# The low parts of three weight blocks move from GpSimd into VectorE's triangular inverse

## What is computed

```python
h = rms_norm(x, norm_g) * (1.0 + scale) + shift
proj = h @ w_in
pool_u, pool_g, q, k, v, ret_g, rw, rw_g, gate_logits = jnp.split(proj, points, axis=-1)
o_pool = causal_pool_mixer(pool_u, pool_w, pool_scale) * jax.nn.silu(pool_g)
o_ret = retention(q, k, v, positions, ret_norm_g) * jax.nn.silu(ret_g)
o_rwkv = rwkv7_time_mix(rw, ...) * jax.nn.silu(rw_g)
...
return x + gate * (merged @ w_out)
```

## Time and profile before

| | |
|---|---|
| three runs | 1833.15, 1835.55, 1838.32 us, median 1835.55 |
| the profiled execution | 1840.28 us, its span 1838.2 us |
| TensorE matmuls busy | 1718.2 us, 93% of the span |
| VectorE busy | 1036.0 us, 56% |
| ScalarE busy | 800.7 us, 44% |
| GpSimd busy | 632.0 us, 34% |
| granted TensorE clock, mean | 0.968 |

### The profile page before, as it was taken

How to read it: one execution, slowest core, us unless ns; L and a number is a source line. 1 busy time by engine, 2 the same in 40 slices (tenths; PEclk the granted TensorE clock), 3 DMA queues, 4 the chain that set the end, 5 groups by cost and what they waited for, 6 DMA issues and landing times. The chain is left out here.

```text
span 1838.2 us, 26011 instructions
## 1 busy us (share of the span) xinstructions
PE 1718.2 (93%) x10688; PEld 1373.8 (75%) x10688; DVE 1036.0 (56%) x1367; ACT 800.7 (44%) x1200; POOL 632.0 (34%) x344
## 2 busy tenths in 40 slices
PE   8999989999999899899999999989999999987783
PEld 6877778888888787688888888868888986544441
DVE  4346744666665325584556766443116627866675
ACT  2455522333223335542333222344337736866673
POOL 1336612424444434751243444433421021322210
PEclk7999989999999899998999999989999999999997
DMA  8223321215444323322122544333420067999994
GB/s 344 81 92 106 90 77 36 92 58 192 171 166 171 126 92 96 96 85 77 54 85 66 209 175 169 138 126 126 149 92 1 1 240 265 382 388 395 389 392 178
DMA packets 82605, 287.97 MB, mean 157 GB/s; under 512 B 30473, under 2 KB 30601, under 8 KB 65332
## 3 DMA queue, kind: packets, MB, share of 16 engines
q1 hardware_dynamic: 76708, 275.87, 41.6%
q0 software_dynamic: 5040, 8.25, 1.4%
q10 hardware_dynamic: 736, 2.14, 0.3%
HBM read 274.50 MB, written 22.61 MB: 162 GB/s over the span
## 5 line engine op out<-in xcount | busy, mean ns | idle before, releaser
L1525 POOL TENSOR_TENSOR wmem_r<-wmem,wmem_r 128x1024 fp32r<-128x1024 f32 x170 | 420.2, 2473 | 696.4 <-ACT wmem_r L1041 685.5
L721 PE MATMUL banks<-h_hi_r,wmem_r 128*128 128x512 f32 x1632 | 511.2, 392 | 6.9 <-POOL wmem_r L1525 6.9
L721 PEld LDWEIGHTS banks<-h_hi_r,wmem_r 128*128 128x128 f32 x1632 | 307.9, 189 | 77.0 <-POOL wmem_r L1525 9.4
L1041 ACT ACTIVATE wmem_r<-wmem 128x1024 fp32r<-128x1024 f32 x170 | 180.2, 1060 | 405.2 <-DMA wmem<-wstream 402.2
L721 PE MATMUL banks<-hT_r,wmem_r 128*128 128x512 f32 x816 | 319.0, 391 | 0.0
L721 PEld LDWEIGHTS banks<-hT_r,wmem_r 128*128 128x128 f32 x816 | 154.0, 189 | 31.3
L2725 DVE TENSOR_TENSOR slots_r<-slots,wmem_r 128x1024 fp32r<-128x1024 f32 x102 | 121.9, 1217 | 57.7 <-ACT wmem_r L2418 52.1
L2806 POOL TENSOR_TENSOR wmem_r<-wmem,wmem_r 128x1024 fp32r<-128x1024 f32 x30 | 74.8, 2493 | 202.3 <-ACT wmem_r L2276 202.3
L992 PE MATMUL banks<-slots_r,wmem_r 128*128 128x512 f32 x512 | 127.7, 389 | 0.0
L1465 DVE SCALAR_TENSOR_TENSOR ztp<-xT,c_act,ztp 128x256 f32<-128x256 f32 x168 | 122.8, 731 | 6.0
L741 PE MATMUL banks<-wmem_r,h_hi_r 128*128 128x512 f32 x384 | 118.9, 391 | 0.0
(11 more groups left out here) (450 smaller groups left out, 3043.1 us busy)
## 6 DMA issues: line engine op xcount, KB each, us to landing
wmem<-wstream SPq DMA_DIRECT2D x206, 512.0 KB, 3.3
slots<-experts SPq DMA_DIRECT2D x80, 1024.0 KB, 24.5
xT<-ada SPq DMA_DIRECT2D x24, 1024.0 KB, 5.8
xT<-experts SPq DMA_DIRECT2D x16, 1024.0 KB, 25.0
slots<-ada SPq DMA_DIRECT2D x8, 1024.0 KB, 18.0
x_keep<-xT SPq DMA_DIRECT2D x2, 2048.0 KB, 17.4
xT<-x_keep SPq DMA_DIRECT2D x2, 2048.0 KB, 8.1
dil_rows<-dil_once SPq DMA_DIRECT2D x1, 2560.0 KB
```

The costliest lines, as they stand in the source:

```text
L721: mm = nc.tensor.matmul(o, r(lhs[:, k, :]), r(rhs[:, k, :]), start=(k == 0 and i == 0), stop=(k == KD - 1 and i == 2))
L1041: inc(nc.scalar.activation(r(chunk(b)[0]), w, ACT.Copy), "w_high")
L1525: inc(g.tensor_tensor(r(lo), lo, r(hi), ALU.subtract), "w_split")
```

## The change

Three of the blocks, rg3 (25), tg0 (26) and tg1 (27), get their low part from VectorE: ahead of the turns i = 13, 20 and 27 of the inverse's loop. GpSimd leaves them out, and a new semaphore `v_split` counts them, for which TensorE waits in place of `w_split`. GpSimd still makes the low parts of rg0, rg1, rg2, tg2 and tg3.

```diff
+LOW_AT = {13: FIRST["rg"] + 3, 20: FIRST["tg"], 27: FIRST["tg"] + 1}
+BY_VECTOR = sorted(LOW_AT.values())
...
-        split_count = lambda b: b + 1 - sum(w <= b for w in WHOLE)
+        high_count = lambda b: b + 1 - sum(w <= b for w in WHOLE)
+        split_count = lambda b: high_count(b) - sum(w <= b for w in BY_VECTOR)
+        split_of = lambda b: ("v_split", BY_VECTOR.index(b) + 1) if b in BY_VECTOR else ("w_split", split_count(b))
...
-                after("w_split", split_count(b))
+                after(*split_of(b))
...
             for i in range(SUB - 1):
+                if i in LOW_AT:
+                    hi, lo = chunk(LOW_AT[i])
+                    after("w_high", high_count(LOW_AT[i]))
+                    inc(v.tensor_tensor(r(lo), lo, r(hi), ALU.subtract), "v_split")
...
-                    if b not in WHOLE:
-                        after("w_high", split_count(b))
+                    if b not in WHOLE and b not in BY_VECTOR:
+                        after("w_high", high_count(b))
```

More of the change, by code:

```diff
@@ L451, in program @@
                           ("o_sqrt", 1), ("ret_done", 4), ("gate_sig", 24), ("merged", 40),
-                          ("w_high", LAYER_B - len(WHOLE)), ("w_split", LAYER_B - len(WHOLE)), ("quarter_used", 9), ("h_high", 8),
+                          ("w_high", LAYER_B - len(WHOLE)), ("w_split", LAYER_B - len(WHOLE) - len(BY_VECTOR)), ("v_split", len(BY_VECTOR)), ("quarter_used", 9), ("h_high", 8),
                           ("br_high", 3), ("br_split", 3), ("m_high", 8), ("m_split", 8)):
@@ L733, in project_tok @@
                     at = FIRST[prefix] + b
-                    after("w_split", split_count(at))
+                    after(*split_of(at))
                     w = [part.rearrange("p (k n) -> p k n", k=2) for part in chunk(at)]
```

## The result

| kernel | median | range, runs | ratio to the kernel before, 95% interval |
|---|---|---|---|
| before | 1837.09 us | 1832.79 to 1839.87, 8 | |
| changed | 1845.47 us | 1840.99 to 1850.59, 8 | 1.0054 [1.0041, 1.0067] |
| changed, a second time | 1846.89 us | 1839.13 to 1849.53, 6 | 1.0061 [1.0042, 1.0080] |

The change makes the kernel slower: by 8.4 us, 0.46%, between the two medians, and by 0.54% in the ratio of the table. The forecast was 4.5 us, and 1840 us. The profiled execution of the changed kernel took 1844.64 us (span 1842.7 us), the one of before 1840.28 us.

A forecast was written before the change was run, and what follows sets the result against it. TensorE's matmuls, busy 93% of the span, were taken as the bound. Net lateness 9.5, plus 1.7 for a clock fall, minus 6.5 of clock returned gave +4.7 us: 1840 us from a median of 1835.55, range 1833 to 1847.

The forecast's parts named there:

- The low parts late: TensorE waits for VectorE's low parts at rg3, tg0 and tg1: 1.55, 2.14 and 3.3 us later, 7.0 us a layer.
- the rival price: By the shared read port rule, each low part on VectorE costs 2.1 us instead of 1.22; no chance given.
- One fall of the clock among dense matmuls: New idle times among the blocks lower TensorE's clock once in the two layers: 1.7 us lost, ends 0 and 3.4.
- What it gives back: Around `zp`: the waits ahead of it go, 2.63 and 1.87 us, and a higher clock returns 6.5 us.
- The covered wait: TensorE's wait ahead of `zp` for the inverse's spread disappears: 2.63 us in the first layer, 1.87 in the second.
- The clock: Without the wait the clock may stay up from `zp` on: 6.5 us back over both layers, ends 0 and 10.
- case 2: Clock falls during small tiles in `zp` and `zc`, wait or no wait: +9.5 to +13 us, 1845 to 1848.5; chance 0.22.
- I carry the difference over unchanged: The +4.7 us on the profiled execution (1840.3 to 1845.0) is applied to the median, 1835.55, giving 1840 us.
- Case 4: Low parts are in time, VectorE's loop running ahead of TensorE: 11 us faster, about 1824.5 us; chance 0.08.

The follow-up runs named there:

- changed, a second time: The changed kernel run again with nothing edited: 1846.89 us, ratio 1.0061 to the kernel before.
- The kernel with other turns: Changed kernel with the three low parts ahead of turns 8, 13 and 18 instead of 13, 20 and 27: 1836.27 us, 0.9997 of before.
- the held pair: Changed kernel and its variant with turns 8, 13 and 18, both with SyncE's three weight loads held until `zc`'s last product: 1844.44 and 1828.27 us.
- A: Not a run: the stretch in TensorE's timeline from rg2's first matmul to `py`, added over both layers; 65.55 us before, 80.89 us changed.
- With the loads held: Changed kernel with SyncE's three weight loads behind the inverse's spread held until `zc`'s last product: 1844.44 us, 1.0045 of before.
- B: Not a run: the stretch from `py` to step 0's first state-update product, added over both layers; 43.90 us before, 34.48 us changed.
- before, second: Second trace of the kernel before, nothing edited: 1835.53 us, ratio 0.9998.
- With them held in both kernels: SyncE's three weight loads held until `zc`'s last product, in the kernel before (1832.90 us) and with turns 8, 13 and 18 (1828.27 us).
- earlier turns for two of three: Changed kernel with rg3's and tg0's low parts at turns 8 and 13, tg1's still at 27: 1852.02 us, 1.0098 of before.
- extra matmuls: Kernel before with eight overwritten 128 x 512 matmuls filling TensorE's wait ahead of `zp`: 1837.75 us; with the three weight loads also held, 1830.83 us.

## Why the prediction fell short

**The low parts late: right.** The waits were said to be about 1.3, 1.9 and 3.1 us, with VectorE as the releaser; they are 1.17, 1.76 and 3.00. The subtraction takes 1.23 us (1.22 said, and 2.1 by the rival price). Late by 7.0 us a layer: from rg2 to `py` the first layer has 39.63 - 32.77 = 6.9 us more. The kernel with other turns shows that it is the place and not the work, and the held pair prices it in the whole kernel's time.

**One fall of the clock among dense matmuls: right,** in either trace, in one layer of the two; A shows it at 1.5 to 1.6 us. With the loads held there were two, so that it was one is partly luck.

**What it gives back: mis-sized,** and this is the step that failed. The forecast took the full wait ahead of `zp`, 2.63 + 1.87 = 4.5 us, and 6.5 us of clock, 11.0 in sum. By two traces of each kernel B falls from (43.90 + 42.63) / 2 = 43.27 to (34.48 + 38.21) / 2 = 36.35 us, that is 6.9 us. With A's 15.34 this makes +8.4 us, the difference first measured (the second was 11.7). The start of `zp` in the timelines cuts B in two. All columns are us, summed over both layers:

| trace | `py` to `zp` | `zp` to the update | full clock lost | idle, issue named |
|---|---|---|---|---|
| before | 17.25 | 26.65 | 13.6 | 1.35 |
| before, second | 14.78 | 27.85 | 6.8 | 5.84 |
| changed | 12.61 | 21.87 | 3.4 | 2.06 |
| changed, second | 12.60 | 25.61 | 8.5 | 3.09 |

- The covered wait, the first column: 3.4 us on average where 4.5 were taken. One execution of before showed waits of 4.5 us, another 2.0, and `zp` starts 6.3 us behind `py` in all four layers of the changed kernel.
- The clock, the second column, which has the late instructions in it too: 3.5 us where 6.5 were taken. The forecast read 13.6 us of lost clock from one execution, and another of the same kernel has half of it. It also let the clock stay up once the wait was gone. No layer of the changed kernel has a wait ahead of `zp`, and the clock falls in `zc` in three of four. What lowers it there is open: it did so with stalls and, with the loads held, without.
- The late instructions, for which there was no term: 1.35 and 5.84 us of such idle before, 2.06 and 3.09 us after.

Layers with no idle time over 0.3 us with issue named, from all fourteen traces, show the clock by itself. From `zp` to the update it is 9.12 us with the clock at full, 11.2 to 11.9 us with 3.4 us of it lost (five layers), and 12.14 and 12.21 us with 5.1 us lost. So to get all of these 5.1 us back is worth some 3 us; the forecast had 4 for that layer.

For the two executions profiled first the forecast was closer: B gave back 9.4 us of the 11.0. That the two differ by 4.4 us in all, where 4.7 were said, is luck in part: A and B make 5.9 of it, and what took the other 1.5 us off is open.

**The row that was not read.** The timeline goes on behind its last row with this one:

```profile
249.43 3.20 PE L856 MATMUL banks<-ztp 32*32 32x32 f32 x111 [1.35 <-issue]
```

The idle of 1.35 us is a stall that neither the wait nor the clock explains, and the forecast has no term for it. Read as "what is late next behind `zp`", it would have been a warning that an earlier or faster `zp` may run into something else; how much that takes can't be read from it.

**The cases.** The time came out in the span of case 2, "the clock gives nothing back". Its mechanism, that the clock falls during the small tiles, wait or no wait, is seen in three of the changed kernel's four layers; but the clock did give something back, fully in the first layer of the first trace. "I carry the difference over unchanged" held for the pair of profiled executions (4.4 us apart, 4.7 said), and misled: the profiled one of before lies above all eight timed runs of it, the profiled one of the changed kernel below its median. What made that execution of before slower outside A and B (109.45 against 108.22 us, of 5.7 us between the two profiled ones) is open.

**Case 4,** the mechanism by which the change would gain, is real, but was priced too high. With the low parts in time by earlier turns the kernel gains nothing (-0.4 us) while the loads are in the way. With them held in both kernels it gains 4.6 us by the medians, 1832.90 to 1828.27, and 5.2 us in A + B; the forecast was 11 us, with no stall counted.

## To carry to other kernels

When work moves into a slower engine's serial loop, set the loop's time from one part to the next against the consumer's time for one block: where the first is longer, each part is later than the one before. Earlier turns for all of them then cost nothing here; earlier turns for two of three made the third later. Before crediting a covered wait or a higher clock, look at the next stall behind it in the same timeline, one with issue named above all, and take a second trace of the same kernel if a wait ahead of a transfer is worth a few microseconds. Loads that are issued long before they are needed are not free when they fall on a stretch of hundreds of small matmuls. Holding them until that stretch was over gained 7 to 8 us by the medians where stalls of 2.2 to 3.3 us stood in it (extra matmuls; turns 8, 13 and 18), and nothing that can be told where the loads were through before it.

## What the runs showed of the hardware

- **TensorE's program is fetched during the run, and the fetch is late behind a burst of loads.** The page of the kernel before has this row among its queues:

```profile
q8 instruction: 88, 1.44, 0.3%
```

88 packets of 16 KB. The Trainium skill (Trainium Architecture — The Big Picture, "The software stack") says that instructions are of 64 bytes and that the streams are moved into each engine's memory when the program is loaded. By the Trainium skill's 64 bytes TensorE's 10688 matmuls and 10688 weight loads are an estimated 1.37 MB, nearly the 1.44 MB of this queue, and a packet is 128 matmuls with their weight loads. The packets during the run differ from what the Trainium skill says there on loading; the measurement decides. That q8 is TensorE's is inferred, from this size, from the stalls 127 matmuls apart, and from the packets ahead of the stalls' ends: in the fourteen traces there are 26 idle times of 0.4 us or more with issue named in stretch B, and each ends 2.2 to 2.9 us behind the start of such a packet. No view names a queue's engine.
- **It limits small matmuls even without loads.** At the full level 126 tiles of 32 x 32 take 2.2 us, and the packets came 3.3 to 4.5 us apart in the traces of before and of the changed kernel; stalls of 0.4 to 1.4 us stayed in the second layer of the changed kernel in all its traces, that with the loads held too. Whether a shorter program for `zp` and `zc` would end them was not tried.
- **The same kernel has different falls of the clock from one execution to the next.** In one trace of the changed kernel all windows from 244 to 264 us are at 1.00; in another they are 0.61 and 0.54 from 248 and 252 us, with the same program and waits. One trace can't tell which falls are usual.
